# Order of the six matmuls of a k-block: products outside and token halves inside, or the other way round

## The reference, cut to what matters

```
xn = rms_norm(x, g1);  z = xn @ w_in + b_in           # 1024 -> 7176 columns: u, q, k, v, o, gates
uc = causal_dwconv(u);  ha = rg_lru(uc)                # branch A, a scan over positions
hb = mlstm(q, k, v, igate, fgate)                      # branch B, 4 heads of 256, in chunks
merged = sigmoid(ga) * (ha @ w_branch_a) + sigmoid(gb) * (hb @ w_branch_b)
x = x + merged @ w_out                                 # 1024 -> 1024
up = rms_norm(x, g2) @ w_up                            # 1024 -> 5632
x = x + (gelu(gate) * val) @ w_down                    # 2816 -> 1024
y = rms_norm(x, g_final)
```

## Time and profile before

| what | value |
|---|---|
| time, median of 3 runs | 1078.87 us (1077.85, 1078.87, 1079.47) |
| the profiled execution: span from first to last instruction, the only time that the profile has of it | 1076.6 us |
| PE busy | 1064.6 us, 99% of the span, 8034 matmuls |
| PEld (weight loads, beside the matmuls) | 1039.3 us, 97%, 8034 loads |
| DVE, ACT, POOL busy | 607.3, 396.8, 369.7 us |
| mean granted TensorE clock | 0.998 of full |
| HBM | 93.56 MB read, 14.83 MB written, 101 GB/s over the span |

### The profile page before, as it was taken

How to read it: one execution, slowest core, us unless ns; L and a number is a source line. 1 busy time by engine, 2 the same in 40 slices (tenths; PEclk the granted TensorE clock), 3 DMA queues, 4 the chain that set the end, 5 groups by cost and what they waited for, 6 DMA issues and landing times.

```text
span 1076.6 us, 19470 instructions
## 1 busy us (share of the span) xinstructions
PE 1064.6 (99%) x8034; PEld 1039.3 (97%) x8034; DVE 607.3 (56%) x959; ACT 396.8 (37%) x574; POOL 369.7 (34%) x179
## 2 busy tenths in 40 slices
PE   7999999999999999999999999999999999999997
PEld 6999999999999999999999999999999999999997
DVE  6777457844343242243443338999950189999412
ACT  6566787313333434322432343222221122222332
POOL 4333334333222222222223344333444244334330
PEclk9999999999999999999999999999999999999999
DMA  8433332236264271363442333232323222223312
GB/s 218 135 106 91 103 81 71 83 103 162 59 183 125 77 224 48 90 204 87 137 164 80 97 86 94 81 93 82 101 59 102 73 79 79 79 84 100 101 45 89
DMA packets 180272, 111.80 MB, mean 104 GB/s; under 512 B 7611, under 2 KB 176811, under 8 KB 179934
## 3 DMA queue, kind: packets, MB, share of 16 engines
q1 hardware_dynamic: 179980, 110.55, 35.6%
q10 hardware_dynamic: 210, 0.07, 0.0%
HBM read 93.56 MB, written 14.83 MB: 101 GB/s over the span
## 4 chain that ended last, share of the span: by engine, by line
PE 98%; ACT 1%; DMA 0%; POOL 0%; DVE 0%; issue 0%; SPq 0%; DVEq 0%
PE ring L1990 48%; PE ring L2420 22%; PE bank L2420 17%; PE bank L2287 2%; PE bank L2274 1%; PE bank L2037 1%; PE bank L2257 1%; PE bank L2267 1%; PE bank L2329 1%; PE bank L2147 1%; PE bank L2317 1%; PE ring L2180 1%; PE bank L2352 0%; DMA x_tok<-in_x_prompt 0%; POOL xl L860 0%; PE bank L2466 0%
## 5 line engine op out<-in xcount | busy, mean ns | idle before, releaser
L848 POOL TENSOR_TENSOR wlo<-stage,whi 128x1024 fp32r<-128x1024 f32 x78 | 194.0, 2487 | 418.8 <-ACT whi L903 418.8
L1990 PE MATMUL ring<-xh,whi 128*128 128x282 f32 (+1 forms) x1008 | 223.7, 303 | 0.0
L1990 PE MATMUL ring<-xl,whi 128*128 128x282 f32 (+1 forms) x1008 | 218.2, 298 | 0.0
L1990 PE MATMUL ring<-xh,wlo 128*128 128x282 f32 (+1 forms) x1008 | 217.7, 297 | 0.0
L1990 PEld LDWEIGHTS ring<-xh,whi 128*128 128x128 f32 x1008 | 162.6, 189 | 8.6 <-issue 8.2
L890 POOL TENSOR_TENSOR wlo<-stage,whi 128x1024 fp32r<-128x1024 f32 (+1 forms) x40 | 109.3, 2734 | 163.9 <-ACT whi L1264 163.9
L1990 PEld LDWEIGHTS ring<-xl,whi 128*128 128x128 f32 x1008 | 163.9, 189 | 0.0
L1990 PEld LDWEIGHTS ring<-xh,wlo 128*128 128x128 f32 x1008 | 163.5, 188 | 0.0
L903 ACT ACTIVATE whi<-stage 128x1024 fp32r<-128x1024 f32 x80 | 84.2, 1053 | 89.3 <-PE ring L1990 81.2
L1264 ACT ACTIVATE whi<-stage 128x1024 fp32r<-128x1024 f32 (+1 forms) x40 | 46.0, 1154 | 101.5 <-PE ring L2420 55.1
L890 POOL TENSOR_TENSOR wlo_third<-stage,whi_third 128x1024 fp32r<-128x1024 f32 (+1 forms) x20 | 52.9, 2643 | 82.4 <-ACT whi_third L1264 82.4
(11 more groups left out here) (377 smaller groups left out, 2256.8 us busy)
## 6 DMA issues: line engine op xcount, KB each, us to landing
stage<-in_w_in SPq DMA_DIRECT2D x56, 512.0 KB, 4.0
stage<-in_w_up SPq DMA_DIRECT2D x44, 512.0 KB, 3.7
stage<-in_w_down SPq DMA_DIRECT2D x16, 704.0 KB, 4.5
stage<-in_w_branch_a SPq DMA_DIRECT2D x8, 512.0 KB, 3.9
c_sample<-in_state_mlstm_C SPq DMA_DIRECT2D x16, 256.0 KB, 6.1
out_s_mlstm_C<-c_sample SPq DMA_DIRECT2D x16, 256.0 KB, 2.4
stage<-in_w_branch_b SPq DMA_DIRECT2D x8, 512.0 KB, 4.0
stage<-in_w_out SPq DMA_DIRECT2D x8, 512.0 KB, 3.8
```

The source lines that it names most:

```text
L848: pool.tensor_tensor(wlo[:, slot, 0:n], stage[:, slot, 0:n], whi[:, slot, 0:n].bitcast(F32), ALU.subtract).then_inc(w_lo, 1)
L1990: last = pe.matmul(of(z, t0, t1), w[:, kk * P:kk * P + P], x[:, kk, t0:t1], start=kk == 0 and m == 0, stop=kk == kn - 1 and m == 2)
```

## The change

In both functions the two inner loops are exchanged. Before, each of the three products of a k-block was done for the first token half and then for the second. Now all three are done for the first half and then all three for the second. Both kernels issue the same matmuls with the same operands, the same first-and-last flags for each bank and the same waits.

```diff
@@ split_product @@
                     if wait_k:
                         wait_k(kk)
-                    for m, (w, x) in enumerate(((wh, xh_), (wh, xl_), (wl, xh_))):
-                        for t0, t1 in halves(m0):
+                    for t0, t1 in halves(m0):
+                        for m, (w, x) in enumerate(((wh, xh_), (wh, xl_), (wl, xh_))):
                             last = pe.matmul(of(z, t0, t1), w[:, kk * P:kk * P + P], x[:, kk, t0:t1],
                                              start=kk == 0 and m == 0, stop=kk == kn - 1 and m == 2)
@@ ffn_steps @@
-                    for m, (w_, x_) in enumerate(((w, xh_), (w, xl_), (l, xh_))):
-                        for t0, t1 in halves(m0):
+                    for t0, t1 in halves(m0):
+                        for m, (w_, x_) in enumerate(((w, xh_), (w, xl_), (l, xh_))):
                             last = pe.matmul(of(z, t0, t1), w_[:, kk * P:kk * P + P], x_[:, kk, t0 - at:t1 - at],
                                              start=kk == 0 and m == 0, stop=kk == kn - 1 and m == 2)
```

## The result

The changed kernel takes 1080.97 us (median of 18 runs, 1079.62 to 1081.88) against 1078.64 us for the kernel before (18 runs, 1077.71 to 1079.69): ratio 1.0019, 95% interval 1.0013 to 1.0025. It is slower by 2.3 us. The effect is small, but its interval doesn't reach 1.0000.

What follows compares the result with a forecast made beforehand. The prediction took TensorE's own matmul-to-matmul steps to bound the kernel. It summed -0.65 us for the banks and 0 for the rest, taking the median from 1078.87 to 1078.2 us, with a range of 1074 to 1083.

Steps and rivals of the forecast that it cites:

- What bounds the kernel: Whole span: PE busy 1064.6 of 1076.6 us, waits on others 6.2 us, all in the opening.
- The banks, -0.65 us: Lines 1990 and 2420: 4640 steps now stay in one bank; two thirds of -0.98 us, good to 4.6 us either way.
- the two pure patterns: Bank changed at every matmul (lines 1990, 2420) and one bank throughout (line 2037); the mixed order was placed between them.
- Within 0.2% of before: Whole kernel: the forecast outcome, 1076.5 to 1081 us, chance 0.60.
- threshold at 0.47: Over 4640 steps, 0.47 ns each makes 2.2 us, the 0.2% a measurement tells from nothing.
- the signs of being wrong: Chain pieces at lines 1990 and 2420 moving by more than 0.5%, or time moving while they don't.
- The weights, 0: Each k-block: four loads of six bring another weight tile instead of two; claimed cost 0.
- The argument by line 2037: At line 2037 two of three loads bring new weights at the plain rate, so more weight changes cost 0.
- The beginning of a tile: Second matmul after other work comes 80 to 100 ns late; no difference taken, 2.8 us at most over 139 tiles.
- The waits and the queues: Waits stay before a block's first matmul and `tile_done` on its last; no buffer, transfer or queue moves.
- a step within one bank costs more: Rival, in PSUM: adding to just-written values meets the draining matmul; 1 ns a step, +4.6 us, 1083.5 us, chance 0.19.
- The clock and the dearer loads: TensorE: clock at 1.00, nothing to win back; loads of new weights dearer, +121 us, 1199 us, chance 0.01.

Runs made afterwards that it cites:

- the bench: Kernel before plus 24 series of 96 extra matmuls in a quiet place; at 280/296 old order 12.59 us, new order 12.69 us.
- the cut of 304: Kernel before with tokens cut at 304 instead of 296: old order 1077.98 us, ratio 0.9994; new order 1076.51 us, ratio 0.9981.
- the bench of single slices: Kernel before plus 37 series of 48 extra matmuls, one weight tile, slices of varied start or length; 288 columns took 6.32 to 6.46 us.
- the one after it: Kernel before plus 34 series of 96 extra matmuls, slice pairs in turn or three and three; 282 columns at 14 took 12.48 us with one bank or two.
- the cut at 304 and 576 tokens: Old-order series of 96 extra matmuls in the kernel before, run in two benches of token cuts: 12.48 us, then 12.74 us.

## Why the prediction was right or wrong

**What bounds the kernel.** This was right. PE's own steps make the time, nobody makes it wait once the large products have begun, and no other engine's work was moved.

**The banks, -0.65 us.** This is the term that failed, and the forecast with it. The bank itself, the thing asked about, is indeed worth nothing (12.59 and 12.60, 12.69 and 12.70). But the term was built on the idea that a step's length is given by its columns and its bank, and two sentences rest on it.

The one that decides is "I take it to lie between the two pure patterns, which agree". The new order doesn't lie between them. At 282/296, the most frequent pair (800 k-blocks of 1160), the bench's step is 133.6 ns in the old order and 133.9 in the new (6.413 and 6.429 us for 48). The two slices repeated alone in one bank take 130.0 and 136.7 (12.48 and 13.12 for 96), or 133.3 in the mean. That is the nearest to a pure one-bank pattern that ran, though its slices don't move on to the next k-block. Both orders are longer than it, and the new one is outside of the two. With slices that don't move on it is outside as well, but on the other side: 133.3 ns in turn (12.80), 133.3 alone, and 132.3 in the new order (12.70). What moved was something that the term didn't hold: the sequence in which slices of different starts and lengths follow.

The other is "With 154.4 a column costs 0.451 ns, and in one bank 296 columns would take 136.4 ns". A straight line was laid through the sizes 256 and 336 and read at 280, 282 and 296, and there is no such line (284 columns cost 1.5 ns more than 288). But the line was off by little at these sizes: 129.1 for a measured 127.8 at 280, 130.0 for 130.0, 136.4 for 136.0 to 136.7. With the measured lengths in its place, and 818 ns for two halves of 296, the same sum would give -0.4 us (an estimate), still with the wrong sign. (The working also has a slip: 3 x 266.4 is 799.2, which is 2.1 and not 2.3 ns below 801.3. That makes -0.55 of the -0.65.)

In place of -0.65 us stand +1.6 us at the changed lines of the traces and +2.3 us between the medians. "Within 0.2% of before" had the largest chance, and 0.19% is just inside of it; as the sum had the other sign, that is luck. The reading was said to be good to 1 ns a step with a threshold at 0.47. The effect is 0.50 ns at line 2420, and it came from outside of what that error covered. Of the signs of being wrong, one showed: a piece of the down projection moved by 0.8% (17.31 to 17.45), though all the named pieces stayed within the lengths given.

**The weights, 0.** This was right, and is now shown for the slices of the up projection: one weight tile for all products changes nothing (6.413 and 6.429 as with two). The argument by line 2037 needed no other size and so wasn't touched by the sequence.

**The beginning of a tile.** Taking nothing was right. The second matmul after other work comes about 0.1 us late in both kernels. In the changed kernel, at the place of the earlier trace rows:

```profile
91.25 0.40 PE L1990 MATMUL ring<-xh,whi 128*128 128x282 f32 x1
91.49 0.29 PE L1990 MATMUL ring<-xl,whi 128*128 128x282 f32 x1
```

**The waits and the queues.** Right; in the rows they are the same but for the two short ones of the opening. (The first half is complete two matmuls earlier than before, not three: its last matmul was the fifth of six and is now the third. Nothing waits for it either way.)

**The rival "a step within one bank costs more".** It had the sign and, with 4.6 us at 1 ns a step, twice the size, but the mechanism is wrong. What spoke for it was that the down projection's steps (131.1 to 132.0) are quicker than the line's 132.7. With the measured lengths that figure is 132.2, which is what the bench's new order takes with either use of the banks (12.69 and 12.70 for 96). The bench's old order takes 131.1 and, with three matmuls to a bank, 131.3 (12.60). The order that this rival calls dear is the faster one at the cut of 304.

**The clock and the dearer loads.** It was right to leave them out. The granted clock is 1.00 in both windows, and there are 8034 loads in both kernels.

What stays open is why a sequence of slices has the length it has. The profile shows starts but not what the array waits for between them. The bench doesn't give the kernel's effect in full detail either. By its settled halves, 100 mixed tiles at 0.016 us and 22 times 48 matmuls of the down projection at 0.05 us make +2.8 us (an estimate), where the traces have +1.6, and what is missing is at line 1990. And of the 2.3 us between the medians, 1.6 are located in the profiled pair. The spans of all runs grew by 1.4 us in the median (1076.8 for 26 runs of the kernel before, 1078.2); the rest is time around the span, which no profile shows.

## What to carry to other kernels

Where TensorE is busy without a gap, the order and the cut of its slices are worth some tenths of a per cent in either direction, and no rule of thumb gives the sign: measure the sequence itself, with its real starts and lengths, before reasoning from another size. To separate two things that an order changes together, such as the bank and the sequence of operands, vary each alone in a series of matmuls put in a quiet place of the kernel; the times of two full kernels agreed here with the wrong theory, and only their tiles taken by kind spoke against it. Try a few even cuts near the middle, multiples of four first (they were the better ones in the old order here, at both numbers of tokens that were tried), and build the best of them, as a bench gives more than the kernel does: 8.1 us promised and 5.4 measured.

## What the runs showed of the hardware that I had not expected

- A float32 slice of the reduced kind, streamed again and again from start 0, takes 119.8 ns at 256 columns, 127.7 at 280, 133.2 at 284, 131.7 at 288 and 136.0 at 296. Counting one column for each period of 2.4 GHz, these would be 106.7, 116.7, 118.3, 120.0 and 123.3 (an estimate). The 11 to 15 ns on top are neither a constant nor a share.
- Where a slice starts in memory changes the step, with all else the same: 288 columns take 131.7 ns from 0 and 134.6 from 14.
- Steps come in rhythms. In the bench of single slices, 280 columns at 0 and 296 at 280 in turn go 124, 136, 124, 136 ns; in the one after it, the slice of 282 at 14 goes 129, 131. Most series of fixed slices there total a multiple of 26.7 ns for 48 settled matmuls (6.240, 6.293, 6.320, 6.347, 6.400 us). That is 3.33 ns for each six matmuls, or 8 periods of 2.4 GHz.
- The same series was seen in two rhythms: 6.09 us for 48 and 12.48 for 96 with 282 columns at 14 in two banks, 12.48 and 12.74 for the cut at 304 and 576 tokens. What had run before differed each time; no run varies that alone.
- Three matmuls in a row that add to the same bank are as quick as three that go to different ones (12.60 and 12.59 us for 96, 12.69 and 12.70).
